# Norm factors spread over 64 features by a matrix product that reads one column 64 times, in a two-block transformer kernel

## The reference

```python
def rms_norm(x, g=None):
    y = x * lax.rsqrt(jnp.mean(jnp.square(x), axis=-1, keepdims=True) + RMS_EPS)
    return y * g
# first block
h = rms_norm(x, norm_mix_g)                        # factor per token
mix, q_mem = rwkv7_time_mix(h, ...)                # 12 heads of 64; inside it:
kk = kk / maximum(sqrt(sum(kk * kk, -1)), 1e-12)   # factor per token and head
y = (y - mean) * rsqrt(var + GN_EPS)               # factor per token and head
mem_out = memory_cross_attention(q_mem, k_mem, ...)  # q and k normed per head
x = x + concatenate([mix, mem_out]) @ w_out
x = x + square(relu(rms_norm(x, norm_ffn_g) @ w_ff1)) @ w_ff2
# second block
h = rms_norm(x, norm_mix_2)
q_a, k_a, v_a, q_b, k_b, v_b, g_a, g_b = split(h @ w_in_2)   # q, k normed per head
# neighbourhood attention (a), sliding window attention (b), gates, w_out_2
x = x + (silu(h2 @ w_gate_2) * (h2 @ w_up_2)) @ w_down_2     # h2 = rms_norm(x, norm_ffn_2)
```

## Time and profile before

| | us |
|---|---|
| median of three runs | 1529.61 |
| the profiled execution, its own time | 1530.44 |
| its span | 1528.5 |
| PE busy in the span | 1467.7 (96%) |
| PE weight loads busy (they overlap PE) | 1158.2 (76%) |
| DVE busy | 811.8 (53%) |
| ACT busy | 548.6 (36%) |
| POOL busy | 239.7 (16%) |

### The profile page before, as it was taken

How to read it: one execution, slowest core, us unless ns; L and a number is a source line. 1 busy time by engine, 2 the same in 40 slices (tenths; PEclk the granted TensorE clock), 3 DMA queues, 4 the chain that set the end, 5 groups by cost and what they waited for, 6 DMA issues and landing times.

```text
span 1528.5 us, 26651 instructions
## 1 busy us (share of the span) xinstructions
PE 1467.7 (96%) x11374; PEld 1158.2 (76%) x11374; DVE 811.8 (53%) x1267; ACT 548.6 (36%) x936; POOL 239.7 (16%) x166
## 2 busy tenths in 40 slices
PE   7998898988999999999999999999999999999999
PEld 5877676756788888888788776667777888888887
DVE  5755667564454453535654357588564443443343
ACT  6544424453332221222442256555233231222221
POOL 0233323311100000000110011312322220220120
PEclk9999999999999999999999999999999999999999
DMA  8311110011133233332232233221223233223223
GB/s 321 111 30 30 35 39 30 30 57 58 44 94 102 91 98 96 96 96 95 85 97 79 86 98 97 77 76 56 78 88 96 85 109 97 87 93 110 84 86 107
DMA packets 39333, 130.88 MB, mean 86 GB/s; under 512 B 4272, under 2 KB 5296, under 8 KB 39216
## 3 DMA queue, kind: packets, MB, share of 16 engines
q1 hardware_dynamic: 39216, 129.18, 26.5%
HBM read 127.07 MB, written 2.10 MB: 85 GB/s over the span
## 4 chain that ended last, share of the span: by engine, by line
PE 80%; DVE 9%; ACT 4%; issue 3%; POOL 0%; POOLq 0%; DVEq 0%; ACTq 0%
PE bank L1048 77%; PE bank L1448 1%; DVE Wlo L1644 1%; ACT Whi L2096 1%; DVE qa L1755 1%; DVE kf L1797 1%; DVE Xi L1892 1%; DVE z L1681 0%; DVE qa L1753 0%; PE bank L1238 0%; PE bank L1162 0%; DVE X L1726 0%; ACT kbr L2335 0%; ACT Hhi L2177 0%; DVE slab L1775 0%
## 5 line engine op out<-in xcount | busy, mean ns | idle before, releaser
L1048 PE MATMUL bank<-Hhi,Whi 128*128 128x512 f32 x912 | 375.3, 412 | 13.5 <-DVE Wlo L1644 10.2
L1048 PE MATMUL bank<-Hhi,Wlo 128*128 128x512 f32 x912 | 361.6, 397 | 0.0
L1048 PE MATMUL bank<-Hlo,Whi 128*128 128x512 f32 x912 | 358.5, 393 | 0.0
L1048 PE MATMUL bank<-Uhi,Whi 128*128 128x512 f32 x736 | 291.5, 396 | 8.5 <-POOL Wlo L2416 3.1
L1048 PE MATMUL bank<-Ulo,Whi 128*128 128x512 f32 x736 | 287.4, 390 | 0.0
L1048 PE MATMUL bank<-Uhi,Wlo 128*128 128x512 f32 x736 | 287.4, 390 | 0.0
L2096 ACT CAST Whi<-Wraw 128x1024 fp32r<-128x1024 f32 (+1 forms) x216 | 223.0, 1036 | 163.6 <-PE bank L1048 147.9
L1644 DVE TENSOR_TENSOR Wlo<-Wraw,Whi 128x1024 fp32r<-128x1024 f32 (+1 forms) x175 | 224.2, 1281 | 99.8 <-ACT Whi L2096 99.7
L1048 PEld LDWEIGHTS bank<-Hhi,Whi 128*128 128x128 f32 x912 | 172.0, 189 | 68.3 <-issue 12.2
L1048 PEld LDWEIGHTS bank<-Hlo,Whi 128*128 128x128 f32 x912 | 172.4, 189 | 42.3
L1048 PEld LDWEIGHTS bank<-Hhi,Wlo 128*128 128x128 f32 x912 | 172.5, 189 | 33.0
(11 more groups left out here) (292 smaller groups left out, 1580.4 us busy)
## 6 DMA issues: line engine op xcount, KB each, us to landing
Wraw<-in_wts SPq DMA_DIRECT2D x208, 512.0 KB, 3.5
bA<-in_biasA SPq DMA_DIRECT2D x12, 256.0 KB, 2.7
Wraw<-in_wts SPq DMA_DIRECT2D x8, 384.0 KB, 3.1
x<-in_xT SPq DMA_DIRECT2D x8, 256.0 KB, 4.5
x_rows<-in_xN SPq DMA_DIRECT2D x2, 1024.0 KB, 7.9
X<-in_xT SPq DMA_DIRECT2D x2, 1024.0 KB, 7.5
out<-X SPq DMA_DIRECT2D x8, 256.0 KB, 2.0
bB<-in_biasB SPq DMA_DIRECT2D x4, 384.0 KB, 3.1
```

Source lines behind the costliest of these rows:

```text
L1048: return e.matmul(o, lhsT, rhs, start=start, stop=stop, skip_group_check=True)
```

## The change

Step 5 is taken away. DVE's work for such a norm ends with the reciprocal. In step 6 PE reads the columns of `st8` themselves: for each group of 128 tokens and each head, one float32 product has a column of `st8` as stationary operand, read 64 times by a stride of zero (128 rows, 64 columns), and the identity as moving operand (128 columns). Its result lands on the 64 partitions of that head. A norm of 512 tokens takes eight such products in place of four transposes. `st8` now lives until PE has read it, so there are four tiles in place of two, and ACT waits before it writes one until the reader of the root four before has finished.

```diff
-    st8 = [sb(f"st8{i}", [128, 8])[:] for i in range(2)]
+    st8 = [sb(f"st8{i}", [128, 8])[:] for i in range(4)]
...
     def small(*root):
-        return st8[N("root", *root) % 2]
+        return st8[(N("root", *root) - 1) % 4]
...
-        def spread(sq, n, root_key, *user):
+        def spread(n, root_key, *user):
             b = bank(*user)
+            x = small(*root_key)
             w.wait_ge(S["wide"], N("root", *root_key))
             for j in range(n // 128):
-                p = e.transpose(b[:, 128 * j:128 * j + 128], sq[:, 128 * j:128 * j + 128], c("ident"))
+                for h in range(2):
+                    by_features = x[:, 2 * j + h:2 * j + h + 1].broadcast_to([128, 64])
+                    p = mm(b[64 * h:64 * h + 64, 128 * j:128 * j + 128], by_features, c("ident"), True, True)
             return p
...
         # VectorE, root
-            own(e.reciprocal(x, x))
-            own_ready()
-            wide = sq[:, 0:n].rearrange("p (j x) -> p j x", x=64)
-            p = e.tensor_copy(wide, x.unsqueeze(2).broadcast_to([128, n // 64, 64]))
             if kind == "m" or key == ("gmix2",):
-                p = e.tensor_copy((rsn if kind == "m" else rsnb)[:, 0:n // 128].unsqueeze(2),
-                                  x.rearrange("p (j h) -> p j h", h=2)[:, :, 0:1])
-            p.then_inc(S["wide"])
+                own(e.reciprocal(x, x))
+                own_ready()
+                e.tensor_copy((rsn if kind == "m" else rsnb)[:, 0:n // 128].unsqueeze(2),
+                              x.rearrange("p (j h) -> p j h", h=2)[:, :, 0:1]).then_inc(S["wide"])
+                return
+            e.reciprocal(x, x).then_inc(S["wide"])
...
         # ScalarE, root
-            w.wait_ge(S["wide"], r - 2)
+            if r > 4:
+                done_with(by_number[r - 4])
```

More of the change, by code:

```diff
@@ L1155, in root @@
             p.then_inc(S["root"])
-        def spread(sq, n, root_key, *user):
+        def spread(n, root_key, *user):
             b = bank(*user)
+            x = small(*root_key)
             w.wait_ge(S["wide"], N("root", *root_key))
             for j in range(n // 128):
-                p = e.transpose(b[:, 128 * j:128 * j + 128], sq[:, 128 * j:128 * j + 128], c("ident"))
+                for h in range(2):
+                    by_features = x[:, 2 * j + h:2 * j + h + 1].broadcast_to([128, 64])
+                    p = mm(b[64 * h:64 * h + 64, 128 * j:128 * j + 128], by_features, c("ident"), True, True)
             return p
         def norm_rows(*name):
-            sq, n = {"x": (acc, T), "m": (accm, 256), "n": (accb, T)}[name[0]]
-            spread(sq, n, name, "rs", *name).then_inc(S["rs"])
+            spread(256 if name[0] == "m" else T, name, "rs", *name).then_inc(S["rs"])
         def head_rows(t):
-            spread(head_square(t), tiles[t].n, ("h", t), "hn", t).then_inc(S["hn"])
+            spread(tiles[t].n, ("h", t), "hn", t).then_inc(S["hn"])
         def key_rows(p):
-            spread(ftmp[plan.F.at["sq", p]], T, ("f", p), "kk", p).then_inc(S["kk"])
+            spread(T, ("f", p), "kk", p).then_inc(S["kk"])
         def group_rows(p):
-            spread(z2, T, ("t", p), "tn", p).then_inc(S["tn"])
+            spread(T, ("t", p), "tn", p).then_inc(S["tn"])
         def decay(p):
@@ L1658, in root @@
         def root(kind, *key):
[L1660 to L1667, removed]
+            n = 256 if kind == "m" else tiles[key[0]].n if kind == "h" else T
             r = N("root", kind, *key)
-            x = st8[(r - 1) % 2][:, 0:n // 64]
+            x = small(kind, *key)[:, 0:n // 64]
             w.wait_ge(S["root_out"], r)
@@ L2117, in mem_token, with done_with @@
             e.activation(memHhi[:, i, :], x, ACT.Copy, scale=v("gmem", i)).then_inc(S["mhi"])
+        by_number = {plan.numbers[x]: x[1:] for x in plan.steps if x[0] == "root"}
+        def done_with(root_key):
+            kind, *key = root_key
+            if kind == "h" and tiles[key[0]].kind in QUERIES:
+                w.wait_ge(S["wide"], N("root", *root_key))
+            else:
+                reader = {"h": "hn", "f": "kk", "t": "tn"}.get(kind, "rs")
+                w.wait_ge(S[reader], N(reader, *(key if reader != "rs" else root_key)))
         def root(kind, *key):
@@ L2127, in root @@
                 one = row_sums[kind].unsqueeze(2).broadcast_to([128, n // 128, 2])
-                e.activation(st8[(r - 1) % 2][:, 0:n // 64].rearrange("p (j x) -> p j x", x=2), one, ACT.Sqrt,
+                e.activation(small(kind, *key)[:, 0:n // 64].rearrange("p (j x) -> p j x", x=2), one, ACT.Sqrt,
                              scale=1.0 / 1024, bias=c("rmseps")).then_inc(S["root_out"])
@@ L2134, in root @@
             scale, bias = {"f": (64.0, None), "t": (1.0, c("gneps"))}.get(kind, (1.0, c("rmseps")))
-            to = st8[(r - 1) % 2][:, 0:n // 64].unsqueeze(2)
+            to = small(kind, *key)[:, 0:n // 64].unsqueeze(2)
             if bias is None:
```

## The result

The changed kernel takes 1537.52 us (median of five runs, 1535.15 to 1538.08); the kernel before, run beside it, 1532.07 (1529.5 to 1532.43). The ratio is 1.0039, 95% interval 1.0025 to 1.0053: slower by 5.5 us on the medians. In a later comparison on another chip the same pair stood at 1.0050, 1.0037 to 1.0063 (1537.48 against 1529.31). The forecast was 1538.7, in a range of 1533 to 1546. The profiled execution has a span of 1535.7 us, 7.2 more than the one before.

The account below looks back on a forecast made before the run. PE was taken as the bound (80% of the chain); terms 1.4 + 0 + 0.5 - 0.3 + 2.35 + 3.95 + 1.2 gave +9.1 us, 1539.5 profiled, 1538.7 on the median. Range: 1533.0 to 1546.0.

Parts of the forecast that it names:

- The price of a group: Spread of 512 tokens between big products: 1.24 us against 0.45, 0.79 more for each of 21 spreads.
- Rival 1: Half-width groups cheap but not free, only doubled slots paid (+0.43 per 512-token spread): +4 us, 1533.6; chance 0.12.
- rival 3: Faster: a group costs no more than four transposes, so only the gains stay: -4.9 us, 1524.7; chance 0.05.
- The stride of zero: Stationary operand of the new products: forecast wrong if it loads at another speed than a stride of one.
- In a full stream nothing hides it: Last tn (386.8 us), accb at 433.7 and three ka: five spreads at 0.79 us, +3.95.
- The two with a chain behind them: accb at 789.2 and kb at 896.7 us, a DVE and ACT chain behind each: about 0.6 each, +1.2.
- Four pairs: Pairs of heads in the mixer: kk +0.57, tn +0.53, ended waits -0.74; net +0.36 us each, +1.4 for four.
- rival 2: Nothing given back: removed copies were not PE's wait, or later y and T become one; +18 us, 1548; chance 0.09.
- First pair: kk spread at 100.8 us: +0.6 on PE, covered by a later 0.70 us idle for DVE's T; taken as 0.
- The start: Up to 60 us, x, first kk, m and last km: +2.35; with -0.3 at 65.08 us, +2.05.
- `accb` at 1167: Spread that waited for the copy; earlier start limited by the big product ahead (0.33 us of wait): +0.25.
- rival 4: PE's clock moves: each low stretch in a full stream costs about 1.7 us; chance 0.02 for several at once.

Follow-up runs that it names:

- e6: Changed kernel with each spread's products issued twice into the same bank; 1554.57 us, ratio 1.0152 to the kernel before.
- e1: Changed kernel, but the x, m and n norms spread by full-width transposes of one st8 column read 128 times; 1534.15 us, ratio 1.0035 to the kernel before.
- e12: Changed kernel with DVE's 24 copies put back ahead of the signal to PE, their output unread; 1539.76 us, ratio 1.0063 to the kernel before.
- e7: Kernel before with the new spread, without copy, only for the twelve kk and tn norms of the mixer; 1531.38 us, ratio 1.0011.
- e9: Kernel before, but ScalarE instead of VectorE makes the copy in the six group norms (tn); 1526.35 us, ratio 0.9981.
- e10: Kernel before with ScalarE's copies in the group norms and copy-free one-column transposes for x, m and n; 1525.07 us, ratio 0.9968.
- e5: Changed kernel with loops over heads and token groups exchanged, four products of one head, then four of the other; 1545.52 us, ratio 1.0098.
- e2: Kernel before, with the reciprocal written straight into the wide tile in place of a small reciprocal and a copy; 1575.02 us, ratio 1.0298.

## Why the prediction was right, and where it wasn't

- **The price of a group.** Forecast 1.24 against 0.45 between big products; measured 1.21 to 1.23. Worked out from four products of the same shape plus weight-load slots. e6 splits it as forecast: 0.87 for the records, 0.35 for the way in and out. Rival 1 left the 0.35 away, rival 3 the second record; both are out. One part of the reading was loose. The 0.34 us between the two big products behind the group were taken as part of its way out. They stand behind four full-width transposes too (434.01 to 434.34 in the earlier trace rows), so they say nothing of the width. What does is the total, 0.35 on top of the records against nothing at full width.
- **The stride of zero**, named as what could make the forecast wrong, costs nothing (e1).
- **In a full stream nothing hides it**: +3.9 for five, forecast 3.95. The two with a chain behind them +1.5, forecast 1.2: hardly anything of the full 0.79 each is hidden.
- **Four pairs, +0.36 each.** Measured +0.38, but the reason given for the third term of 0.57 + 0.53 - 0.74 is wrong. I said that the wait for `Xi` goes since DVE is free of the copy. e12 has the copy, and the wait is gone as well: the spread itself became 0.5 us longer and `Xi` no longer was the later one. A given-back wait and a longer group ahead of it were the same 0.7 us, and either removed it. For the same reason rival 2, nothing given back, can't come out at +18: with every copy kept the kernel stands at 1.0063, +10.5 on the medians.
- **First pair**: 0, as forecast; the 0.67 was taken back in the wait of the earlier trace rows.
- **The start**: +1.3 for a forecast of +2.05. The largest part of the gap is the gain at 65 us, 0.8 where I took 0.3; `qm` came 0.2 earlier as well.
- **`accb` at 1167**: forecast +0.25, measured +0.25 and then -0.6. I had not read the wait for `Wlo` ten us later. PE and DVE there before:

```profile
1173.00 0.69 DVE L1768 TENSOR_TENSOR qa<-bank,RSb 128x512 f32<-128x512 f32 x1 [2.48 <-POOL qa L2429]
...
1178.03 0.50 PE L1048 MATMUL bank<-Uhi,Whi 128*128 128x512 f32 x1 [0.86 <-DVE Wlo L1644]
```

  and after:

```profile
1180.38 0.69 DVE L1762 TENSOR_TENSOR qa<-bank,RSb 128x512 f32<-128x512 f32 x1 [2.13 <-POOL qa L2435]
...
1185.42 0.50 PE L1048 MATMUL bank<-Uhi,Whi 128*128 128x512 f32 x1 [0.28 <-DVE Wlo L1646]
```

  From the reciprocal to the end of that `Wlo`, over DVE, ACT and POOL, are 10.70 us in the changed kernel, in e1, e7, e9 and e10, with the copy or without, with the short group or the long one. PE waits for this chain in all of them. So at this place the longer group is hidden, and a shorter one gains nothing: e1 and e10 wait 0.97 us. Before, the chain took 11.05, as `qa` waited 0.35 us longer for POOL. These 0.35 are the whole net gain here, and they are not shown to be the change's, since e7 and e9 have the old spread and copy here and gain them too. What lies behind a stage must be read for each spread, not only for those with a known wait.
- **The clock** (rival 4) moved the profiled executions by single stretches, as said, in both directions. It accounts for -1.1 us here, and for most of what differs between executions of one kernel. That the medians stand at +5.5 in one comparison and +8.2 in the other, with places that sum to +8.0, I put down to it; that is argued from the traces, not shown for the unprofiled runs.

## What to carry to other kernels

Removing work from an engine that PE rarely waits for pays only at the places where PE waits; moving the same work onto PE, the bound, is paid at each. Before you trade a copy for more products, count the groups that stand in a full stream and price them by an existing group of the same shape. Then ask which part of the removed work was really waited for, and whether an idle engine can take just that: here six copies of 24, on ScalarE, gave 3 us where the change cost 5 to 8. And a wait that seems to go because its cause was removed may go because something ahead of it grew; a run with the cause put back tells.

## What the runs showed of the hardware that was new

- Products on the two halves of the columns overlap even when all of one half stand ahead of all of the other: the second half began 0.49 us after the first, which ran for 0.87 (e5).
- A DVE reciprocal of 128x512 takes 3.35 us, 6.3 ns per column (e2), and POOL doesn't hold it up, where a copy is held up from 0.43 to 1.67.
- A stationary operand that reads one column 128 times takes no longer than a plain one: 0.45 us for a group of four transposes (e1).
- A group of half-width products between full-width ones costs some 0.35 us beyond its records (1.23 us for sixteen, 2.10 for thirty-two in e6); four float32 products of full width cost 0.91 us for eight records at 0.11, nothing beyond.
- The stretches of low clock come and go between executions of the same kernel and shift it by up to 1.7 us each: two traced executions of the changed kernel had them at 321, 352 and 406 us, and at 292, 322 and 1036.
